# Products of ones into a free bank at seven places where TensorE waits, in a one-core kernel of two transformer blocks

## The reference

```
mix = even_mixer_2(x, ...) if l % 2 == 0 else odd_mixer(x, ...)
x = layer_norm_2(ALPHA * x + mix, ln_g[l, 0], ln_b[l, 0])
ffn = routed_moe(x, router_w, router_b, moe_w_gate[l], moe_w_up[l], moe_w_down[l])
x = layer_norm_2(ALPHA * x + ffn, ln_g[l, 1], ln_b[l, 1])
```

## Time and profile before

| | before |
|---|---|
| time, median of 3 runs | 2475.62 us (2473.22 to 2476.98) |
| the profiled execution | 2474.83 us, span 2472.9 us |
| mean granted clock of TensorE | 0.973 |
| TensorE busy, products | 2328.4 us, 94% of the span |
| VectorE, ScalarE, GpSimd busy | 1740.1, 1197.9, 115.7 us |

### The profile page before, as it was taken

How to read it: one execution, slowest core, us unless ns; L and a number is a source line. 1 busy time by engine, 2 the same in 40 slices (tenths; PEclk the granted TensorE clock), 3 DMA queues, 4 the chain that set the end, 5 groups by cost and what they waited for, 6 DMA issues and landing times.

```text
span 2472.9 us, 33815 instructions
## 1 busy us (share of the span) xinstructions
PE 2328.4 (94%) x14128; PEld 2038.2 (82%) x14128; DVE 1740.1 (70%) x2355; ACT 1197.9 (48%) x1549; POOL 115.7 (5%) x205
## 2 busy tenths in 40 slices
PE   7999999899989999999999998979999888899997
PEld 3778888778779999998999997868888687688886
DVE  4997777754776666666666655668888777688886
ACT  3222222334544454455554443457666555576665
POOL 0111111010000000000000010000000100000000
PEclk9999999999999999999999998989999989999999
DMA  7777887433115454455445552239988621389884
GB/s 273 230 243 254 269 265 262 130 132 110 69 58 182 171 205 169 172 205 216 153 160 177 180 199 102 99 108 330 349 311 316 259 103 52 124 341 345 317 311 167
DMA packets 80533, 501.71 MB, mean 203 GB/s; under 512 B 9584, under 2 KB 10688, under 8 KB 28656
## 3 DMA queue, kind: packets, MB, share of 16 engines
q1 hardware_dynamic: 59120, 423.66, 46.7%
q0 software_dynamic: 21248, 75.75, 9.7%
HBM read 498.33 MB, written 1.05 MB: 202 GB/s over the span
## 4 chain that ended last, share of the span: by engine, by line
PE 61%; DVE 22%; ACT 11%; issue 4%; DMA 2%; DVEq 0%; SPq 0%; ACTq 0%
PE bank L412 60%; DVE wl L2076 9%; ACT wh L1410 7%; DVE macc L2112 1%; ACT s L1511 1%; DVE f L2293 1%; DMA mring<-in_wmod 1%; DVE s L2284 1%; DMA raw<-in_wmod 1%; PE bank L1282 1%; DMA raw<-in_wstream 1%; DVE rs L2136 1%; PE bank L649 0%; DVE hl L2268 0%; DVE st_od L2343 0%
## 5 line engine op out<-in xcount | busy, mean ns | idle before, releaser
L2076 DVE TENSOR_TENSOR wl<-raw,wh 128x2048 fp32r<-128x2048 f32 (+1 forms) x437 | 905.0, 2077 | 378.1 <-ACT wh L1410 374.1
L1410 ACT ACTIVATE wh<-raw 128x2048 fp32r<-128x2048 f32 (+1 forms) x437 | 756.3, 1738 | 301.3 <-PE bank L412 295.1
L412 PE MATMUL bank<-hh,wh 128*128 128x258 f32 (+2 forms) x2200 | 691.7, 314 | 34.2 <-ACT o_rl L1839 5.3
L412 PE MATMUL bank<-hh,wl 128*128 128x258 f32 (+2 forms) x2200 | 675.2, 307 | 0.0
L412 PE MATMUL bank<-hl,wh 128*128 128x258 f32 (+2 forms) x2200 | 673.9, 306 | 0.0
L412 PEld LDWEIGHTS bank<-hh,wh 128*128 128x128 f32 x2200 | 422.1, 192 | 63.8 <-DVE hl L2714 6.0
L412 PEld LDWEIGHTS bank<-hl,wh 128*128 128x128 f32 x2200 | 422.6, 192 | 18.2 <-issue 0.5
L412 PEld LDWEIGHTS bank<-hh,wl 128*128 128x128 f32 x2200 | 421.1, 191 | 18.8
L412 PE MATMUL bank<-wh,hh 128*128 128x512 f32 (+1 forms) x704 | 279.2, 397 | 7.6 <-DVE wl L2076 4.7
L412 PE MATMUL bank<-wl,hh 128*128 128x512 f32 (+1 forms) x704 | 276.2, 392 | 0.0
L412 PE MATMUL bank<-wh,hl 128*128 128x512 f32 (+1 forms) x704 | 276.2, 392 | 0.0
(11 more groups left out here) (471 smaller groups left out, 2644.8 us busy)
## 6 DMA issues: line engine op xcount, KB each, us to landing
raw<-in_wstream SPq DMA_DIRECT2D x393, 1024.0 KB, 4.8
mring<-in_wmod POOLq DMA_DIRECT2D x128, 512.0 KB, 4.6
raw<-in_wmod SPq DMA_DIRECT2D x6, 1024.0 KB, 7.4
X<-in_xT SPq DMA_DIRECT2D x1, 2048.0 KB, 13.4
mods<-in_wmod SPq DMA_DIRECT2D x2, 1024.0 KB, 20.0
bias<-in_nabias POOLq DMA_DIRECT2D x16, 128.0 KB, 2.5
c_sglg<-in_sglg POOLq DMA_DIRECT2D x1, 1024.0 KB, 5.0
c_sglb<-in_sglb POOLq DMA_DIRECT2D x1, 1024.0 KB, 7.5
```

The costliest lines, as they stand in the source:

```text
L412: return e.matmul(out, lhsT, rhs, start=start, stop=stop, skip_group_check=True)
L1410: e.activation(wh[i % NB][:, o], raw[i % NR][:, o], ACT.Copy).then_inc(*slab_high(st.split + m))
L2076: e.tensor_tensor(wl[i % NB][:, o], raw[i % NR][:, o], wh[i % NB][:, o].bitcast(F32), ALU.subtract).then_inc(*slab_low(st.split + m))
```

## The change

The change adds `fill(n)` at seven places of TensorE's program, with the default of 256 columns. Two of the places run once, four run once in each router, and one runs in each layer norm, so that 52 products of ones are added in all: 8 ahead of the outer products, 8 ahead of the odd mixer, 1 in each of four layer norms, and in each of two routers 6 ahead of the products with `c_rw`, 4 ahead of the ranks, 2 ahead of the flag and 4 ahead of the last scatter. There the banks 2 to 7 are kept out of its choice, so that it writes bank 0 or 1. No other engine's program changes.

```
         def layer_norm(i):
+            fill(1)
             square_sums(7 + i, T)
...
+            fill(8)
             for n, u in enumerate(pairs):
                 outer(n, u)
...
+            fill(8)
             p(2, 8, "ocq")
             p(1, 10, "ock")
...
             b = bank(("aff", l), act_out, "aff", l)
             w.wait_ge(const_in[f"rw{l}"], 0)
+            fill(6)
             for k in range(KC):
                 w.wait_ge(act_out, "ln x", nm, k)
...
             b = bank(("rank", l), dve_out, "flag", l)
+            fill(4)
             w.wait_ge(dve_out, "gates", l)
...
+            fill(2)
             w.wait_ge(dve_out, "flag", l)
             was = (result.count, dict(w.heard), dict(st.drain), st.tile, len(order))
...
             w.heard = {s: min(n, heard[s]) for s, n in w.heard.items() if s in heard}
+            st.kept.update(range(2, 8))
+            fill(4)
+            st.kept.difference_update(range(2, 8))
             scatter(3, 2)
```

## The result

The changed kernel takes 2470.32 us (median of 12 runs, 2461.25 to 2473.79), the kernel before on the same chip 2475.75 (12 runs, 2471.91 to 2480.09). The ratio is 0.9976 with a 95% interval of 0.9967 to 0.9984: 5.4 us in the medians, and between 4 and 8 us faster by the interval. The forecast of 2468.7 lies 1.6 us under it, and the time is inside the range. Its profiled execution has a span of 2470.8 us, a mean clock of 0.980 (0.973 before), and products on TensorE for 2343.5 us, 15 more than before: the 52 added ones are some 22 us (an estimate, 52 x 0.43), less what the others got shorter.

A forecast was written before the change was run, and what follows sets the result against it. TensorE, busy 94% of the span, bounds by where it runs slowly or stands. Terms 2.2 + 0.65 - 0.4 + 1.9 + 1.5 + 0.3 + 0 = 6.15 us, from 2474.83, gave 2468.7 us; range 2463.8 to 2472.9.

The forecast's parts named there:

- The products are hidden in the waits: At the filled waits except the flag's, products of ones at 0.43 us each fit inside at the full clock.
- They hold the clock: Products of ones keep TensorE's clock at 1.00 over the waits; older, half as wide ones had not hindered it.
- Router, ranks: Router's products 2.2 us and VectorE's wait for the ranks 0.65 us shorter in the first layer, 0 in the second.
- rival C: More than summed: other executions may lose 2.2 us at the second router; 11 us gain, 2463.8, chance 0.09.
- Flag, -0.4: Ahead of the flag's load: waiting for an empty product queue delays the gather 0.2 us per layer, bounds 0 and -0.8.
- Gather, 1.9: Gather at full clock takes 5.7 us: 1.0 us gained in the first layer, 0.9 in the second, bounds 0 and 2.75.
- rival B: The clock's fall only moves to thin work behind the waits; some 2.5 us gain, 2472.3, chance 0.21.
- Scatter, 1.5: In the scatter, VectorE's waits for TensorE at the half clock go, both layers: 1.5 us, bounds 0 and 1.5.
- Outer products, 0.3 of at most 0.45: VectorE's 16 additions set the pace at 5.99 us; only the 0.45 us ahead can shrink, gain 0.3.
- Odd mixer, 0 of at most 1.8: The clock still falls, later, where TensorE goes at VectorE's pace: gain taken 0, at best 1.8 us.
- Layer norms, 0: One product in each layer norm, 0.43 us in a wait of 0.97: hidden, no gain.
- Rule on transposes: If transposes do not count as busy, the gather gains nothing and the run takes 1.9 us more, 2470.6.

The follow-up runs named there:

- the other kernel: The whole change without the six products ahead of each router: 2469.14 us against 2473.24 for the kernel before, ratio 0.9986.
- one behind each block: The whole change plus one 128-column product of ones behind each of the odd mixer's first eight blocks: 2467.32 us against 2476.24 before, ratio 0.9961.

## Why the prediction was right, point by point

- **The products are hidden in the waits.** Right. The waits of the earlier trace rows are shorter by what was put in, and nothing behind them starts later in the changed kernel. The price of 0.43 us each was right too (six products took 2.75 us and twelve 5.34, 0.43 for each of the six more). Twelve ahead of the router showed what too many would do: the router starts 1.2 to 1.3 us later.
- **They hold the clock.** Right, and now shown at the outer products (1.00 in six kernels of six with them, 5.64 or 5.65 us for 6.41 and 6.42 without) and at the router (4.06 us or less to the sigmoid in all twelve cases; without them slow in three of four). With 4 columns in their place the gain is gone. At gather and scatter they hold it only part of the time.
- **Router, ranks.** 2.13 and 0.68 us for 2.2 and 0.65. The forecast gave the second router nothing, as it was fast already; that was this execution's luck. Without products it was slow in the other kernel too (5.34 us), so that the routers are worth 2.8 us over the profiles. This is what rival C said, which got 0.09.
- **Flag, -0.4.** Wrong in a cost that isn't there: the load comes 0.6 us behind the ranks' read with an empty queue and with products still running in it. The two products cost something in one case only, 0.15 us, where they ran at the half clock (one behind each block, second layer).
- **Gather, 1.9.** 1.33. The forecast was whole in the first layer and half in the second. In fact the clock fell in both, on thin work between sigmoid and gather, as rival B has it: with 4 and 2 products the gather was short in 5 of 8 cases, with 6 and 3 in 4 of 4, which are few to tell the two apart. A short one takes 5.82 to 6.03 us; the 5.7 of the forecast was never reached. The first layer's part was mis-sized (1.0, measured 0.15), the second's was near (0.9, measured 1.2).
- **Scatter, 1.5.** 1.75 in the pair, 0.9 over the profiles. In the changed kernel VectorE's waits for TensorE, named by the earlier trace rows, are gone; in four others the clock fell later in the stage and brought one back, of 0.12 to 0.48 us. That the clock holds through the scatter was taken as certain, and it isn't.
- **Outer products, 0.3 of at most 0.45.** Here a step failed: "VectorE's 16 additions take 5.99 us without a pause and set the pace". They take 5.50 at the full clock. One addition takes 0.35 us in both kernels:

```profile
L2523 DVE SCALAR_TENSOR_TENSOR mCT<-mCT,mAPB,bank x16: 344/349/351, 667.8 to 673.5; 128x129 f32<-128x129 f32 x16
```

In the changed kernel the sixteen follow one another in 5.50 us; most of the 0.5 more of before were short waits, of up to 0.14 us each, which the timeline doesn't print. So the term was mis-sized: measured 0.86, outside the bound. A row of the timeline without idle time doesn't show that its engine sets the pace. Multiply the duration of one instruction by their number and compare.

- **Odd mixer, 0 of at most 1.8.** Right. The 0.55 of the pair is inside the spread of the profiles, and the mechanism is right: the clock fell inside the paced stretch (1974.6), and with a product behind each block it did not.
- **Layer norms, 0.** Right where it can be seen: with the single product and none ahead of the router, the time from the sum to the router's first product is that of before (10.6 and 10.0 us). The other two norms weren't tried apart.
- **Rule on transposes.** The Trainium skill, TensorE: Matmul & The Clock Gate, Part 4: PE-mode transpose, has it that transposes do not count as busy in the same way. In the second layer of before the clock stayed at 1.00 behind 16 transposes. That one row speaks against the rule; no run tested it.
- **The sum.** 6.15 for 5.4 in the medians, with an interval from 4 to 8 that also holds the 7.2 of the pair and the 7.3 of the means; the runs can't tell these apart. The forecast is right in its mechanism, but that the sum came within 1 us of the medians has luck in it: over the profiles the scatter gave 0.6 us less than forecast, and the flag 0.4, outer products and routers 0.6 each more; and stretches that the change doesn't touch vary by as much as its gain.

## What to carry to other kernels

Where the records show the half clock behind a wait in which TensorE has nothing to do, and the work behind the wait is on the chain, fill it with products like those of this kernel (256 columns, 128 rows) into a bank that is free, as many as fit at the full clock. Look at the whole chain of waits, not at the longest: the clock can fall at the next thin stretch as it did before, and where TensorE goes block by block at another engine's pace, as in the odd mixer, eight small products between the blocks did what eight wide ones ahead of them did not. Judge the change by the stages around it, in several profiles; here the spread of untouched stretches was larger than the gain.

## What was not expected of the hardware

Products of 32 rows and products of 128 rows occupy TensorE for nearly the same time (3.71 and 3.62 us for eight), but only the latter kept the clock up ahead of the outer products (six profiles; one with 32 rows). And a register load on TensorE ran 0.75 us ahead of the end of products queued before it (1637.7 against 1638.45).
